# Block A's mask pairs inside the dot groups, slot numbers turned early, and Pool building half of block B's weighted masks

## The reference, cut to what matters

```python
def conformer_conv(x, w_in, b_in, w_dw, b_dw, ln_g, ln_b, w_out, b_out):
    h = x @ w_in + b_in
    a, gate = jnp.split(h, 2, axis=-1)
    h = a * jax.nn.sigmoid(gate)
    h = causal_depthwise_conv(h, w_dw, width=31) + b_dw
    h = jax.nn.swish(layer_norm(h, ln_g, ln_b))      # norm over the 2048 channels
    return h @ w_out + b_out

def peer(x, w_q, sub_keys, u_tab, v_tab):            # 8 heads, 2 x 128 sub-keys, 16384 experts
    q = (x @ w_q).reshape(n_tok, 8, 2, 128)
    top_s, top_i = lax.top_k(einsum("thcd,hckd->thck", q, sub_keys), 16)
    best_s, best_j = lax.top_k(all 16 x 16 sums of top_s, 16)
    experts = take(top_i[..0] * 128 + top_i[..1], best_j)     # 8 x 16 = 128 slots a token
    gates = softmax(best_s)
    h = einsum("thkd,td->thk", u_tab[experts], x)             # 128 dots of 2048 a token
    coef = gates * gelu(h)
    return einsum("thk,thkd->td", coef, v_tab[experts])

# each layer: x = layer_norm(2**0.5 * x + mixer(x)); x = layer_norm(2**0.5 * x + peer(x, ...))
```

## Time and profile before

| | |
|---|---|
| median of three runs | 3607.17 us |
| the profiled execution's own time | 3611.92 us |
| its span | 3610.0 us |
| mean granted TensorE clock | 0.908 |
| busy: TensorE / VectorE / ScalarE / POOL | 81% / 71% / 22% / 53% |
| chain that ended last | DMA 41%, PE 24%, DVE 20%, issue 9%, POOL 4%, ACT 1% |

### The profile page before, as it was taken

The page is one execution under the profiler, slowest core; times in us unless marked ns, Lnnn a source line. Parts: engine busy times, 40 slices in busy tenths (PEclk is TensorE's granted clock), DMA queues, the critical chain, the costliest instruction groups (busy, mean ns, idle before and its releaser), DMA issues.

```text
span 3610.0 us, 46542 instructions
## 1 busy us (share of the span) xinstructions
PE 2933.5 (81%) x15209; PEld 2256.1 (62%) x15209; DVE 2580.9 (71%) x3472; ACT 810.2 (22%) x1215; POOL 1910.6 (53%) x1526
## 2 busy tenths in 40 slices
PE   8977895767777789999399998957767777899994
PEld 7864695666767654444198886956666776544441
DVE  4997669787888776666744455697878887766667
ACT  1002431222333420000033443312223334300000
POOL 6795165777777554444300001547777775644443
PEclk9986997888989899999799999978889898999997
DMA  7421446999999669999855435459999997699998
GB/s 248 140 93 41 169 140 253 422 419 422 421 421 422 260 258 410 406 409 409 324 177 186 145 110 183 140 225 423 422 422 421 421 422 283 245 409 406 409 410 319
DMA packets 293734, 1106.84 MB, mean 307 GB/s; under 512 B 21957, under 2 KB 120837, under 8 KB 220677
## 3 DMA queue, kind: packets, MB, share of 16 engines
q0 software_dynamic: 147456, 805.37, 55.1%
q1 hardware_dynamic: 146182, 300.22, 23.1%
HBM read 1103.41 MB, written 2.10 MB: 306 GB/s over the span
## 4 chain that ended last, share of the span: by engine, by line
DMA 41%; PE 24%; DVE 20%; issue 9%; POOL 4%; ACT 1%; DVEq 0%; POOLq 0%; ACTq 0%; SPq 0%
DMA ring<-in_peer_u,index_now 21%; DMA work<-in_peer_v,index_add 14%; PE ps L631 8%; PE ps L651 7%; DMA more_add<-in_peer_v,index_add 6%; DVE work L1218 6%; DVE ps L1467 4%; PE ps L810 3%; POOL ring L544 3%; DVE ring L1424 2%; DVE x_tok L1309 1%; DVE hot_set L1487 1%; PE ps L695 1%; DVE work L1373 1%; DVE work L1370 1%
## 5 line engine op out<-in xcount | busy, mean ns | idle before, releaser
L1424 DVE SCALAR_TENSOR_TENSOR ring<-ring,x_tok 128x2048 f32<-128x2048 f32 x384 | 879.7, 2299 | 229.2 <-DMA ring<-in_peer_u,index_now 221.3
L544 POOL DMA_INDIRECT ring<-in_peer_u,index_now x512 | 843.2, 1647 | 367.1 <-issue 114.9
L849 PE MATMUL ps<-all_v,mix 128*128 128x512 f32 x1984 | 851.8, 592 | 0.0
L849 PEld LDWEIGHTS ps<-all_v,mix 128*128 128x128 f32 x1984 | 377.0, 190 | 474.5 <-issue 474.5
L816 PE MATMUL ps<-x_dot,work 128*128 128x128 f32 x4096 | 536.4, 294 | 94.3 <-ACT work L1066 65.6
L1467 DVE SCALAR_TENSOR_TENSOR ps<-work,coef,ps 128x1024 f32<-128x1024 f32 x344 | 442.2, 1289 | 233.1 <-DMA work<-in_peer_v,index_add 231.3
L810 PE MATMUL ps<-ident,ring 128*128 128x128 f32 x2048 | 348.4, 342 | 311.7 <-DMA ring<-in_peer_u,index_now 306.1
L816 PEld LDWEIGHTS ps<-x_dot,work 128*128 128x128 f32 x4096 | 518.9, 209 | 115.3 <-ACT work L1066 79.8
L810 PEld LDWEIGHTS ps<-ident,ring 128*128 128x128 f32 x2048 | 310.8, 179 | 333.8 <-DMA ring<-in_peer_u,index_now 194.7
L508 POOL TENSOR_TENSOR w_lo<-ring,w_hi 128x2048 fp32r<-128x2048 f32 x34 | 159.2, 4686 | 662.5 <-ACT w_hi L947 662.5
L590 POOL DMA_INDIRECT work<-in_peer_v,index_add x312 | 295.2, 946 | 316.9 <-DVE ps L1467 257.3
(11 more groups left out here) (183 smaller groups left out, 3682.3 us busy)
## 6 DMA issues: line engine op xcount, KB each, us to landing
all_v<-in_peer_v SPq DMA_DIRECT2D x248, 512.0 KB, 6.8
ring<-in_conv_w_in SPq DMA_DIRECT2D x16, 2048.0 KB, 8.8
ring<-in_peer_w_q SPq DMA_DIRECT2D x16, 2048.0 KB, 8.6
ring<-in_attn_w_kv SPq DMA_DIRECT2D x16, 2048.0 KB, 8.6
ring<-in_conv_w_out SPq DMA_DIRECT2D x8, 2048.0 KB, 7.9
ring<-in_attn_w_q SPq DMA_DIRECT2D x8, 2048.0 KB, 8.6
ring<-in_attn_w_o SPq DMA_DIRECT2D x8, 2048.0 KB, 7.9
ring<-in_peer_u,index_now POOLq DMA_INDIRECT x512, 15.0
```

What stands on the lines that cost most here:

```text
L544: pool.indirect_dma_start(u_tile(s), None, u_tab, bass.IndirectOffsetOnAxis(ap=index_now[:, half, s:s + 1], axis=0)).then_inc(u_row[s], 16)
L849: mm = pe.matmul(ps[:, dense_bank(tb, q), :], mix[tb][:, row, :], tile[:, q * 512 - HALF:(q + 1) * 512 - HALF], start=False, stop=True, sk ...
L1424: dve.scalar_tensor_tensor(out=u_tile(s), in0=u_tile(s), scalar=1.0, in1=x_tok[:, tb, :], op0=ALU.mult, op1=ALU.mult, accum_out=coef[:, tb ...
```

## The change

1. `TURNED` is (1, 5) instead of (3, 7).
2. Block A's 16 pairs stand before groups 2 to 15: two pairs before each of groups 2 and 3 (`DOUBLE` = 2), one before each of groups 4 to 15, none behind.
3. The numbers of both blocks are transposed and copied early in block B's dots (`turn_numbers`, `take_numbers`); only `coef` is turned late (`turn_coef`, `take_coef`). VectorE's wait for the residual stands in front of the first add, behind the masks of round 0.
4. Block B's rounds: VectorE makes three masks of 512 elements (both masks of set 0 and of set 1, and the unweighted one of sets 2 and 3 together); POOL makes the weighted mask of sets 2 and 3 by itself, with four instructions of 128 elements.
5. `FIRST_ADDS` is 16: each of the 16 rounds has one add and one gather.
6. The residual and bias of the convolution stand behind the 12th of the 16 pairs of sums.

```diff
-TURNED = (3, 7)
+TURNED = (1, 5)
-FIRST_ADDS = 10
+FIRST_ADDS = 16
+DOUBLE = 2
+EARLY_SUMS = 12
@@ gpsimd, block B's rounds
-                        pool.wait_ge(set_made, layer * ROUNDS * SETS + n + 1)
-                        pool.tensor_tensor(out=hot_set[:, m, 0, :, :], in0=hot_set[:, m, 0, :, :],
-                                           in1=by_slot[:, 1, 2, n * PAIR:(n + 1) * PAIR].unsqueeze(2).to_broadcast([P, PAIR, P]),
-                                           op=ALU.mult).then_inc(set_weighed_pool, 1)
+                        pool.wait_ge(set_used, layer * ROUNDS * SETS + n + 1)
+                        for k in range(PAIR):
+                            t = n * PAIR + k
+                            last = pool.tensor_scalar(hot_set[:, m, 0, k, :], iota_f[:, :], by_slot[:, 1, 0, t:t + 1], by_slot[:, 1, 2, t:t + 1],
+                                                      ALU.is_equal, ALU.mult)
+                        last.then_inc(set_weighed_pool, 1)
@@ tensor, convolution
-            pe.wait_ge(glu_done, 4 + KC)
-            pe.wait_ge(bias_loaded, 16)
-            for b in range(6):
-                residual_bias(b // Q, b % Q)
             pe.wait_ge(ch_steps, 1)
             for n, k in enumerate(CONV_ORDER):
+                if n == EARLY_SUMS:
+                    pe.wait_ge(glu_done, 4 + KC)
+                    pe.wait_ge(bias_loaded, 16)
+                    for b in range(6):
+                        residual_bias(b // Q, b % Q)
@@ tensor, mixer
+                def turn_numbers():
+                    pe.wait_ge(route[layer], part_at(1, 1) + PART_INDEX)
+                    for tb in range(TB):
+                        for c in range(2):
+                            mm = pe.transpose(ps[:, tb, c * P:(c + 1) * P], row_e[:, tb, c, :], ident[:, :])
+                        mm.then_inc(numbers_ready, 1)
+                def turn_coef(tb):
+                    pe.wait_ge(numbers_taken, (layer + 1) * TB)
+                    pe.wait_ge(coef_done, layer * TB + tb + 1)
+                    pe.transpose(ps[:, coef_bank(tb), 0:P], coef[:, tb, :], ident[:, :]).then_inc(slot_ready, 1)
@@ tensor, block B's rounds (mix_round)
+                        if m == SETS // 2:
+                            pe.wait_ge(set_masked, i + (layer * ROUNDS + 1))
@@ tensor, order
                 turned_dots(1, 0)
-                turn_slots(0)
+                turn_numbers()
                 turned_dots(1, 1)
-                with pe.Fori(0, GROUPS - 2) as i:
-                    mix_pair(i)
+                turn_coef(0)
+                with pe.Fori(0, DOUBLE) as i:
+                    for off in range(2):
+                        mix_pair(i, 2, off)
                     turned_dots(1, i + 2)
-                with pe.Fori(GROUPS - 2, BATCHES // 2) as i:
-                    mix_pair(i)
-                turn_slots(1)
+                with pe.Fori(2 * DOUBLE, GROUPS) as i:
+                    mix_pair(i, 1, 0)
+                    turned_dots(1, i)
+                turn_coef(1)
@@ vector, masks of block B, and order
+                def mask_round(r):
+                    for m in range(SETS // 2):
+                        n = r * SETS + m
+                        t = n * PAIR
+                        dve.wait_ge(set_used, layer * ROUNDS * SETS + n + 1)
+                        dve.tensor_tensor(...).then_inc(set_made, 1)
+                    ...
+                    dve.wait_ge(set_used, layer * ROUNDS * SETS + (r + 1) * SETS)
+                    dve.tensor_tensor(out=hot_set[:, SETS // 2:SETS, 1, :, :], ...).then_inc(set_masked, 1)
...
-                dve.wait_ge(slot_taken, layer * TB + 1)
-                for b in range(BATCHES):
-                    masks(b)
-                    if b < 28 and b % 2:
-                        dots(1, 2 + b // 2, 3 + b // 2)
+                dve.wait_ge(numbers_taken, layer * TB + 1)
+                for p in range(BATCHES // 2):
+                    masks(2 * p)
+                    masks(2 * p + 1)
+                    if p >= 2 * DOUBLE:
+                        dots(1, p, p + 1)
+                    elif p % 2:
+                        dots(1, 2 + p // 2, 3 + p // 2)
+                dve.wait_ge(numbers_taken, (layer + 1) * TB)
+                dve.wait_ge(mix_ready, (layer + 1) * BATCHES)
                 for e in range(NT):
                     last_dot(1, e)
                 weights(1)
+                mask_round(0)
-                dve.wait_ge(slot_taken, layer * TB + 2)
-                dve.wait_ge(x_scaled, (layer + 1) * TB)
-                dve.wait_ge(mix_ready, (layer + 1) * BATCHES)
                 for n in range(ROUNDS):
-                    for m in range(SETS):
-                        mask_set(n, m)
+                    if n:
+                        mask_round(n)
+                    else:
+                        dve.wait_ge(x_scaled, (layer + 1) * TB)
                     if n < FIRST_ADDS:
                         add(...)
```

More of the change, by code:

```diff
@@ L258, in build @@
         set_made, set_weighed, set_weighed_pool = sem("set_made"), sem("set_weighed"), sem("set_weighed_pool")
-        set_used = sem("set_used")
+        set_used, set_masked = sem("set_used"), sem("set_masked")
+        numbers_ready, numbers_taken = sem("numbers_ready"), sem("numbers_taken")
         mix_ready, mix_taken = sem("mix_ready"), sem("mix_taken")
@@ L318, in dense_bank, with coef_bank @@
             return Q * tb + q
-        def slot_bank(tb):
+        def coef_bank(tb):
             return (Q + 2) * tb
@@ L1023, in peer, with take_numbers, gelu_of @@
                         exp_of(layer, 0, 0)
-                def take_slots(tb):
+                def take_numbers():
+                    for tb in range(TB):
+                        act.wait_ge(numbers_ready, layer * TB + tb + 1)
+                        act.activation(by_slot[:, tb, 0:2, :], ps[:, tb, 0:2 * P].rearrange("p (a b) -> p a b", a=2), ACT.Copy) \
+                           .then_inc(numbers_taken, 1)
+                def gelu_of(tb):
                     n = layer * TB + tb
@@ L1079, in peer, with weigh_pair @@
                 take_turned(1, 0)
-                take_slots(0)
+                gelu_of(0)
+                take_numbers()
+                take_turned(1, 1)
+                take_coef(0)
                 act.wait_ge(slot_taken, layer * TB + 1)
-                take_turned(1, 1)
                 made = layer * 2 * BATCHES
-                def weigh_pair(i):
+                def weigh_pair(i, step, off):
                     for b in range(2):
-                        act.wait_ge(hot_made, i * 4 + (made + 2 * b + 2))
-                        weigh_hot(i, b)
+                        act.wait_ge(hot_made, i * (4 * step) + (made + 4 * off + 2 * b + 2))
+                        weigh_hot(i, step, off, b)
                         if b:
-                            take_mix(0, i, 0)
-                    take_mix(0, i, 1)
-                with act.Fori(0, GROUPS - 2) as i:
-                    weigh_pair(i)
-                    take_turned(1, i + 2)
-                with act.Fori(GROUPS - 2, BATCHES // 2) as i:
-                    weigh_pair(i)
-                take_slots(1)
+                            take_pair(i, step, off, 0)
+                    take_pair(i, step, off, 1)
+                with act.Fori(0, DOUBLE) as i:
+                    for off in range(2):
+                        weigh_pair(i, 2, off)
+                    take_turned(1, i + 2)
+                with act.Fori(2 * DOUBLE, GROUPS) as i:
+                    weigh_pair(i, 1, 0)
+                    take_turned(1, i)
+                gelu_of(1)
+                take_coef(1)
                 act.wait_ge(slot_taken, layer * TB + 2)
                 def weigh_set(i, m):
-                    act.wait_ge(set_made, i * SETS + (layer * ROUNDS * SETS + m + 1))
+                    act.wait_ge(set_made, i * (SETS // 2) + (layer * ROUNDS * (SETS // 2) + m + 1))
                     for k in range(PAIR):
@@ L1479, in masks @@
                                           op=ALU.is_equal).then_inc(hot_made, 1)
[L1481 to L1488 removed]
+                def mask_round(r):
[3 more added lines that the diff above has]
+                        dve.wait_ge(set_used, layer * ROUNDS * SETS + n + 1)
+                        dve.tensor_tensor(out=hot_set[:, m, :, :, :], in0=iota_f[:, :].unsqueeze(1).unsqueeze(1).to_broadcast([P, 2, PAIR, P]),
+                                          in1=by_slot[:, 1, 0:2, t:t + PAIR].unsqueeze(3).to_broadcast([P, 2, PAIR, P]),
+                                          op=ALU.is_equal).then_inc(set_made, 1)
+                    t = (r * SETS + SETS // 2) * PAIR
+                    numbers = by_slot[:, 1, 1, t:t + SETS // 2 * PAIR].rearrange("p (m k) -> p m k", m=SETS // 2)
+                    dve.wait_ge(set_used, layer * ROUNDS * SETS + (r + 1) * SETS)
+                    dve.tensor_tensor(out=hot_set[:, SETS // 2:SETS, 1, :, :],
```

(3 more changed lines are left out.)

53 lines of the change are left out of this document (20 added, 33 removed).

## The result

The changed kernel took 3617.97 us (median of 14 runs, 3613.19 to 3623.74), the kernel before 3609.03 us beside it (14 runs, 3604.32 to 3616.77): ratio 1.0021, interval [1.0013, 1.0029], that is 0.2% slower. The forecast was 3562 us. The profiled execution of the changed kernel has a span of 3614.6 us against 3610.0.

The account below looks back on a forecast made before the run. Bound taken as DMA bandwidth in U's fetches and the dense product, small instructions with VectorE busy between; -8.5 - 14.8 - 12.8 - 2 x 7.5 + 2 x 1 + 2 x 2 = -45.1 us, giving 3562 us, range 3545 to 3592.

Parts of the forecast that it names:

- Rounds: Block B's rounds: POOL's mask instruction 0.45 us, a round 3.8 us, 61 us against 59, 1 us more a layer.
- Rival D: Block B's rounds: POOL's comparison costs L474's 1.09 us, 6.66 us a round, 46 us more a layer, 3654 us; chance 0.08.
- Hand-over: Last fetched tile's landing (t) to first add: t + 8.1 instead of t + 22.9 and t + 20.9, gaining 14.8 and 12.8 us.
- U: Dots over fetches of U: moved mask pairs delay the freeing of buffers, 2 us a layer lost, bounds 0 and 8.
- The reserve of 3.5 to 8.5 us: Fetch queue at the double groups: landings 9.0 to 14.0 us after issue against 5.5, to hide 6 us of delay.
- Adds: Behind the dense product: six more adds inside the rounds gain 7.5 us a layer, bounds 0 and 10.
- Convolution: Convolution's statistics: mean out 9.7 us earlier, projection near 329 instead of 337.3, gain 8.5 us, bounds 5 and 10.
- 4.0 a bank: Convolution: two banks of residual and bias left before the projection on TensorE take 8 us, from 321 to 329.

Follow-up runs that it names:

- Experiment 5: Changed kernel with POOL's masks of block B covering only the first 64 of 128 columns, the others zero: 3595.65 us, one run.
- experiment 2: Changed kernel with POOL's comparison replaced by a subtraction in the same instruction: 3619.53 us, ratio 1.0017 to the kernel before.
- experiment 1: Changed kernel with VectorE making both masks of all four sets again, POOL only weighting, 16 adds kept: 3578.77 us, ratio 0.9904 to the kernel before.
- The square: Changed kernel with old masks, block A's pairs spread or last, slots (1, 5) or (3, 7): spread 3578.77, 3581.80 us; last 3598.24, 3591.75 us.
- experiment 3: Changed kernel with ten instead of sixteen adds in the rounds: 3623.21 us, ratio 1.0032 to the kernel before.
- experiment 6: Changed kernel with constants in place of the two scalars POOL's masks read from memory: 3583.20 us, one run.

## Why the prediction was wrong

*Rounds: the step that failed.* "I take 0.45: L484's form, stretched by 1.6." The instruction took 0.78 at its shortest and 0.997 in the mean, four of them 4.03 us and not 1.8. The steady round was put at 3.8 us and is 5.27. That the issue took 1.03 us and not the 1.87 of the earlier trace rows helped by 0.84 and hid part of it. The number came from halving L484's 0.553 for 256 elements. Experiment 5 doesn't bear out the halving, since 0.36 of 0.78 us doesn't go with the columns. Nor does L484 fit that split, by which its 256 columns would take 1.2 us. Load from VectorE doesn't separate L484 from the dear row L474 either. At their first use VectorE stood idle for the 11.89 us before 49.59:

```profile
38.10 0.55 POOL L484 TENSOR_SCALAR work<-work 128x256 f32<-128x256 f32 x1 [34.70 <-DVE work L1203]
38.63 1.83 POOL L474 TENSOR_SCALAR work<-work 128x256 f32<-128x256 f32 x2
...
49.59 0.48 DVE L1195 SCALAR_TENSOR_TENSOR work<-ps,vec,work 128x256 f32<-128x256 f32 x1 [11.89 <-ACT work L968]
```

L474 took 0.92 to 0.93 us in its seven records there, with no VectorE instruction beside them, and 1.09 in the median of its 120 records; L484 took 0.553 in all four of its records, three of them with a VectorE instruction running. Why L484 is so short stays open. It was four records that no other row of this engine supported.

*Rival D had the right place and nearly the right size.* It had the point from which it decides: "a round of 5.2 us, an instruction of 0.7 us". The measured 5.27 and 1.0 lie past it, and the kernel is slower by 0.2%. Its reason, the comparison, was not the cause (experiment 2). Its own number, 3654, came from 6.66 us a round, with L474's full 1.09, the long issue and a wait of 0.43; the gaps in the measured round are 0.21 together. It was given 0.08, though L474 was as near to the new instruction as L484.

*There was little to win.* Undisturbed rounds of before start 3.60 us apart (the first masks at 1239.00, the add at 1241.42 for 1.28 in the earlier trace rows, the next masks at 1242.61), and with the disturbed ones an old round with an add takes 3.9 us (experiment 1). The forecast round of 3.8 gains 1 to 2 us a layer against that, its lower bound of 3.56 some 5. The forecast itself claimed nothing here: it set 61 us against the 59 of before, where six rounds had no add.

*Hand-over: right.* Forecast t + 8.1, measured t + 7.5 in both layers, 28.8 us gained against 27.6. The square shows that this gain is one of two edits together.

*U: mis-sized.* 2 us a layer were taken, bounds 0 and 8; it is 4.5 and 5.4 in the trace of the changed kernel, and 4.3 and 8.6 in the square. The reserve of 3.5 to 8.5 us by landing times was not one: runs with the doubled pairs at a deeper queue lose as much. And the effect of `TURNED`, said to be "inside the same reserve", costs U 1 to 5 us by single traces.

*Adds: right behind the rounds.* 20.0 us were gained there against 15, of which experiment 3 gives 17.4 to the adds. From TensorE's last product to the first statistic layer 0 takes 24.7 us, 28 forecast and 36 before. The same six adds cost 8.6 us in the rounds. The forecast had an issue of POOL in every round for it, but no price of its own, so the 15 are not what the adds are worth: that is 8.8 us in the changed kernel and 6.1 with the old masks.

*Convolution: right, low.* 11.9 us in the trace and 9 alone, 8.5 forecast. The mean was forecast 9.7 us earlier, and the way of it was right; they were 11.9, because the last chunk itself was squared 1.85 us earlier (317.54 against 319.39). The term "4.0 a bank", by which the forecast came down to 8.5, was read at a granted clock of 0.50; behind the mean, at 1.00, a bank took 2.1 us and cost nothing.

*The clock* was in no term. TensorE's products of the rounds take 434 ns in the mean at 0.53 of the clock, 325 before. POOL is busy for all but 0.21 us of a round, so a round isn't longer for it; but the residual before the dense product takes 6.42 and 5.54 us instead of 3.70, 2.7 and 1.8 us of the 26. In experiment 6, with rounds of 3.92 us and POOL at 2.70, the clock is 1.00 from 1230 to 1280; in experiment 5, with rounds of 4.3 to 4.9 us, it is 0.64 from 1240 to 1260. That the slower rounds themselves bring the clock down fits all three and was not tried by itself.

## What to carry to other kernels

Where two rows of an engine disagree by a factor of two on what a new instruction costs, carry both prices through the sum until it is known why they differ; a cheap row of four records is the weaker one. Work moved from the bounding engine to another helps only down to the other's sum, so write both sums for one period, and take the old period from the starts of many rounds in the timeline, not from the mean of one instruction. Where two waits end at nearly the same time, removing either alone can lose: test the pair.

## What the runs showed that was not expected

POOL's `tensor_scalar` of 128 columns with two scalars from memory takes 0.78 us when nothing stands against it: about 0.42 for the columns, 0.15 for the scalars and 0.21 that neither explains (experiments 5 and 6). The old form, a multiplication of 256 columns with the coefficients as a second operand, takes 0.62 us in the median of experiment 1, that is 0.31 for each 128 x 128 mask, but it only weights a mask that VectorE has made. L484, with 256 columns in 0.553 us, fits neither.

POOL's and VectorE's masks stretch each other, and which of the two pays varies. In 26 of the 32 rounds of the changed kernel the POOL mask that starts 0.33 us into VectorE's pair takes 1.53 us and the pair 1.28. In the third round of each layer one starts at the same distance, takes 1.02, and the pair takes 1.54. VectorE's single mask, which starts 0.08 us behind a POOL mask, takes 0.98 us in 28 of 32 rounds and 0.69 to 0.72 in the others. In experiment 6 the POOL mask takes 0.71 us and the pair 1.51. In experiment 1 all masks of VectorE over 0.9 us stand beside POOL's multiplication. What decides who pays is not shown.
